# Head norms by a product with a block of ones, modulation columns by transposes, experts gathered by twos

## What is computed

```python
def rms_norm(x, g):                       # over a head (64 or 256 wide) or a latent (256, 128)
    y = x * lax.rsqrt(jnp.mean(x * x, axis=-1, keepdims=True) + EPS)
    return y * g
D_MODEL, SEQ, DEPTH, N_ADA = 1024, 256, 2, 9
N_EXPERTS, TOP_K, EXPERT_FF = 8, 2, 3584  # each of 256 tokens goes to its two best experts
```

## Time and profile before

| | |
|---|---|
| runs | 3294.65, 3297.51, 3300.77 us |
| profiled execution | 3293.94 us, span 3292.1 us |
| mean granted TensorE clock | 0.963 |
| TensorE busy | 3153.1 us, 96% |
| VectorE, ScalarE busy | 2261.7 us (69%), 1701.9 us (52%) |
| read from HBM | 734.95 MB |

### The profile page before, as it was taken

One profiled execution on the slowest core, in us unless ns is written; L12 is line 12 of the kernel. 1 busy time (PEld: TensorE's weight loads), 2 busy tenths in 40 slices (PEclk: granted clock), 3 DMA queues, 4 the chain that ended last, 5 costly groups with the idle time before them and its releaser, 6 DMA issues.

```text
span 3292.1 us, 49368 instructions
## 1 busy us (share of the span) xinstructions
PE 3153.1 (96%) x21206; PEld 2908.7 (88%) x21206; DVE 2261.7 (69%) x2574; ACT 1701.9 (52%) x1910; POOL 84.8 (3%) x163
## 2 busy tenths in 40 slices
PE   6999899999998999999989999999999999989999
PEld 6999899999988998899978888888888888889999
DVE  6686667677555555454575888888888888544575
ACT  4434343443534335443434777777777777444453
POOL 1010001011000000000000000000000000000000
PEclk9999899999988999999987999999999999989999
DMA  7685458678421653245412988989889889423353
GB/s 278 239 305 206 145 193 289 221 278 293 171 71 65 218 203 124 70 144 184 167 39 88 368 338 341 363 338 362 342 337 365 337 341 364 153 103 129 104 192 116
DMA packets 112319, 739.26 MB, mean 225 GB/s; under 512 B 12480, under 2 KB 12480, under 8 KB 32096
## 3 DMA queue, kind: packets, MB, share of 16 engines
q1 hardware_dynamic: 89424, 651.21, 53.1%
q0 software_dynamic: 22672, 84.84, 7.2%
HBM read 734.95 MB, written 1.05 MB: 224 GB/s over the span
## 4 chain that ended last, share of the span: by engine, by line
PE 79%; DVE 5%; ACT 2%; issue 1%; DMA 0%; DVEq 0%; ACTq 0%; POOLq 0%
PE ps L514 60%; PE ps L513 17%; PE ps L523 2%; DVE wlo L2702 2%; DVE AF L2684 1%; ACT whi L1823 1%; DVE att L2693 0%; DVE hl L2675 0%; DVE gf L2687 0%; ACT cv L1811 0%; DVE T L2675 0%; DVE AF L2675 0%; ACT hh L1811 0%; ACT L1811 0%; ACT AF L1811 0%
## 5 line engine op out<-in xcount | busy, mean ns | idle before, releaser
L2702 DVE TENSOR_TENSOR wlo<-ring,whi 128x2048 fp32r<-128x2048 f32 x620 | 1418.7, 2291 | 505.9 <-ACT whi L1823 505.5
L1823 ACT ACTIVATE whi<-ring 128x2048 fp32r<-128x2048 f32 x620 | 1186.0, 1915 | 342.9 <-issue 236.0
L514 PE MATMUL ps<-whi,AR 128*128 128x512 f32 (+1 forms) x2724 | 880.2, 398 | 0.4 <-DVE AF L2675 0.4
L514 PE MATMUL ps<-hh,whi 128*128 128x256 f32 x2464 | 707.5, 287 | 3.9 <-DVE wlo L2702 3.3
L514 PE MATMUL ps<-hl,whi 128*128 128x256 f32 x2464 | 701.3, 285 | 0.0
L514 PE MATMUL ps<-hh,wlo 128*128 128x256 f32 x2464 | 701.3, 285 | 0.0
L514 PEld LDWEIGHTS ps<-whi,AR 128*128 128x128 f32 x2724 | 511.7, 188 | 117.9 <-DVE AF L2675 0.9
L514 PE MATMUL ps<-wlo,AR 128*128 128x512 f32 (+1 forms) x1362 | 536.9, 394 | 0.0
L514 PEld LDWEIGHTS ps<-hh,whi 128*128 128x128 f32 x2464 | 476.1, 193 | 8.6 <-DVE wlo L2702 3.5
L514 PEld LDWEIGHTS ps<-hl,whi 128*128 128x128 f32 x2464 | 476.3, 193 | 0.1
L514 PEld LDWEIGHTS ps<-hh,wlo 128*128 128x128 f32 x2464 | 475.6, 193 | 0.2
(11 more groups left out here) (218 smaller groups left out, 3322.1 us busy)
## 6 DMA issues: line engine op xcount, KB each, us to landing
ring<-in_w SPq DMA_DIRECT2D x620, 1024.0 KB, 4.9
rring<-in_r POOLq DMA_DIRECT2D x151, 512.0 KB, 4.7
AF<-in_mem POOLq DMA_DIRECT2D x2, 1024.0 KB, 6.1
X<-in_x POOLq DMA_DIRECT2D x1, 1024.0 KB, 14.0
AF<-in_cst POOLq DMA_DIRECT2D x1, 1024.0 KB, 5.4
y_out<-X SPq DMA_DIRECT2D x1, 1024.0 KB, 3.8
cst<-in_cst POOLq DMA_DIRECT2D x1, 608.5 KB, 4.4
sm<-in_small POOLq DMA_DIRECT2D x1, 378.0 KB, 4.6
```

What stands on the lines that cost most here:

```text
L514: return self.e.matmul(out, l, r, start=start, stop=stop)
L1823: self.e.activation(N.whi[:, c % HB, :], N.ring[:, c % RING, :], ACT.Copy).then_inc(N.sem["hi"], 1)
L2702: self.e.tensor_tensor(N.wlo[:, c % HB, :], N.ring[:, c % RING, :], N.whi[:, c % HB, :].bitcast(F32), ALU.subtract).then_inc(N.sem["lo"], 1)
```

## The change

- Head norms: one matmul with a 128x128 block matrix of ones (`pairs`, or all ones in `cross` and `hybrid`) gives the sums already spread over the partitions; root and reciprocal then work over the whole tile, in place, in one of three slots of `gs`. `rows_of`, `bcast`, `rows_out`, `rT` go.
- Modulation columns: four transposes and a reduction on VectorE in place of the four matmuls with a column of ones.
- Experts: one selection matrix for two experts; `gather` is run for pairs, with 256 columns per matmul, and the first slice of an odd expert comes before the even one's matmuls back.
- A constant `SLOTS = 3` is put before `LOADS`, and used for the slots of `gs`. `SLOTS = 128` (L24), `experts` and `second` are not in the diff.

```diff
@@ constants
-    put("ex", ex.reshape(4, -1))
+    put("pairs", (i[:, None] // 64 == i[None, :] // 64).astype(np.float32))
@@ -130,6 +126,7 @@
+SLOTS = 3
 LOADS = ("cst", "small", "x", "mem", "pos", "rot3", "pool3", "mem3")
@@ Net
-        self.gs = sb("gs", [P, 2, 512])
+        self.gs = sb("gs", [P, SLOTS, 512])
@@ lay
-        self.e_zeh, self.e_zel = ar.take(8, P), ar.take(8, P)
-        self.e_Sel = ar.take(2, P)
+        self.e_Sel = ar.take(2, 2 * P)
         self.o_Sel = ar.take(2, P)
         af = Arena(self.AF)
         af.n = ar.n
+        self.e_zeh, self.e_zel = ar.take(2, 8, P), ar.take(2, 8, P)
@@ Side
+    def slot(self, key):
+        return self.N.gs[:, self.count.slots[key] % SLOTS, :]
@@ Pe
+    def wide_sum(self, key, weights, tiles, last=1):
+        b = self.take((key, "ss"))
+        self.wait_ge("act", (key, "sq", last))
+        for k, x in enumerate(tiles):
+            t = self.mm(b[:, 0:x.shape[-1]], weights, x, k == 0, k == len(tiles) - 1)
+        t.then_inc(*self.up((key, "ss")))
@@ Pe.ada_sums
         for i in range(4):
-            t = self.mm(b[:, i:i + 1], self.acc[:, g % 2, i * P:(i + 1) * P], N.ones[:, 0:1], True, True)
+            t = self.tr(b[:, i * P:(i + 1) * P], self.acc[:, g % 2, i * P:(i + 1) * P])
@@ Pe.pair_stat
-        self.stat(key, [sq[:, 0:S], sq[:, S:2 * S]], self.N.C("half"))
+        self.wide_sum(key, self.N.C("pairs"), [self.next_slot(key)])
@@ Pe.gather
-        for g in range(2):
+        for g in range(4):
             for lo, z in enumerate((N.hh2, N.hl2)):
                 b = self.take((ex, "ze", g, lo))
-                for j in range(4):
-                    k = 4 * g + j
+                for j in range(2):
+                    k = 2 * g + j
                     for tb in range(2):
-                        t = self.mm(b[:, j * P:(j + 1) * P], z[:, tb, k * P:(k + 1) * P], Sel[:, tb, :], tb == 0, tb == 1)
+                        t = self.mm(b[:, j * S:(j + 1) * S], z[:, tb, k * P:(k + 1) * P], Sel[:, tb, :], tb == 0, tb == 1)
@@ Pe.expert
-        up(0)
-        up(1)
+        if ex % 2 == 0:
+            up(ex, 0)
+        up(ex, 1)
...
-        if ex < 7:
+        if ex % 2 == 0:
+            up(ex + 1, 0)
+        elif ex < 7:
             self.gather(ex + 1)
@@ Act
+    def wide_root(self, key, div, out=None):
+        out = self.slot(key) if out is None else out
+        self.wait_ge("mm", (key, "ss"))
+        self.act(out, self.ps((key, "ss"))[:, 0:out.shape[-1]], ACT.Sqrt, (key, "sqrt"), ("free", (key, "ss")), scale=1.0 / div,
+                 bias=self.N.C("eps"))
@@ Act.pair_squares
-        if r >= 2:
-            self.wait_ge("mm", (self.sqs[r - 2], "ss"))
+        if r >= SLOTS:
+            self.wait_ge("dve", (self.sqs[r - SLOTS], "h", 1))
@@ Dve.ada_sums
-        self.tt(N.mod[:, l, m], self.ps(("ada", g))[:, 0:4], N.V("ada_b", l)[:, m], ALU.add, ("free", ("ada", g)))
+        turned = self.ps(("ada", g)).rearrange("p (a b) -> p a b", a=4)
+        self.e.tensor_reduce(out=cols, in_=turned, axis=AX, op=ALU.add).then_inc(*self.up(("free", ("ada", g))))
+        self.wait_ge("dve", self.here())
+        self.tt(cols, cols, N.V("ada_b", l)[:, m], ALU.add)
@@ Dve
+    def wide_inv(self, key, out=None):
+        out = self.slot(key) if out is None else out
+        self.wait_ge("act", (key, "sqrt"))
+        self.rec(out, out, (key, "inv"))
@@ Dve.pair
+        inv = self.slot(key)
+        self.wait_ge("dve", (key, "inv"))
         for k in range(2):
-            self.stt(x[:, k, :], x[:, k, :], gain, self.ps(bc)[:, 0:S], ALU.mult, ALU.mult, (key, "h", k), ("free", bc))
+            self.stt(x[:, k, :], x[:, k, :], gain, inv[:, k * S:(k + 1) * S], ALU.mult, ALU.mult, (key, "h", k))
@@ Dve.select, two experts at a time
+        for i in range(2):
+            for tb in range(2):
+                at = slice(ex + i, ex + i + 1)
+                self.ts(N.e_Sel[:, tb, i * P:(i + 1) * P], N.C("iota")[:, 0:P], RK[:, tb, at], M[:, tb, at], ALU.is_equal,
+                        ALU.mult, *([(ex, "sel")] if i and tb else []))
```

More of the change, by code:

```diff
@@ L294, in lay @@
         af.n = ar.n
+        self.e_zeh, self.e_zel = ar.take(2, 8, P), ar.take(2, 8, P)
+        self.e_gh, self.e_gl = ar.take(3, 256), ar.take(3, 256)
+        self.e_SelT = [ar.take(S) for _ in range(4)]
+        self.e_yh, self.e_yl = ar.take(1024), ar.take(1024)
+        assert ar.n <= self.AF.shape[1]
         self.o_w = [af.take(CH), flat2(self.T)]
@@ L403, in __init__ @@
         self.seen, self.held = {}, {}
-        self.row, self.rt, self.base, self.span = {}, {}, 4, 4
+        self.row, self.base, self.span = {}, 4, 4
         self.sq, self.sqs = 0, []
@@ L564, in start, with stat @@
         self.wait_ge("act", "consts")
-    def stat(self, key, tiles, inds=None):
+    def stat(self, key, tiles):
         n = len(tiles)
@@ L570, in stat, with stat_part @@
         self.take((key, "ss"))
-        self.stat_part(key, tiles, range(n), inds)
-    def stat_part(self, key, tiles, part, inds=None):
+        self.stat_part(key, tiles, range(n))
+    def stat_part(self, key, tiles, part):
         n, b = len(tiles), self.ps((key, "ss"))
@@ L942, in hybrid @@
         self.lin(("hy", "u", 0), [(0, name, (0,), 0, 8, (0, 256))], "hy")
-        self.stat("hyq", [T4[:, k, :] for k in range(2)])
-        self.stat("hykv", [N.T[:, 0, :]])
+        self.wide_sum("hyq", N.ones[:, :], [T4[:, k, :] for k in range(2)])
+        self.wide_sum("hykv", N.ones[:, :], [N.T[:, 0, :]], 0)
         self.lin(("hy", "gc", 0), [(0, name, (0,), 0, 8, (512, 256))], "hy")
@@ L1169, in nsa, with next_slot @@
         self.new_x()
[L1171 to L1176, removed]
-    def pair_stat(self, key):
-        sq = self.N.gs[:, self.sq % 2, :]
-        self.sq += 1
-        self.stat(key, [sq[:, 0:S], sq[:, S:2 * S]], self.N.C("half"))
[L1185 to L1190, removed]
+    def next_slot(self, key):
+        self.count.slots[key] = self.sq
+        self.sq += 1
+        return self.slot(key)
+    def pair_stat(self, key):
+        self.wide_sum(key, self.N.C("pairs"), [self.next_slot(key)])
     def memory(self):
@@ L1370, in conv_layer @@
         lin("g", 0)
-        self.stat("cvm", [N.T[:, k, :] for k in range(2)], N.C("half"))
+        self.wide_sum("cvm", N.C("pairs"), [flat2(N.T[:, 0:2, :])])
         lin("a", 0)
-        self.pair_rows("cvm")
         lin("g", 1)
-        self.pair_bcast("cvm")
         lin("a", 1)
@@ L2617, in cross @@
         lin("k", 1)
-        self.root("k0", 256)
+        self.wide_root("k0", 256, self.slot("k0")[:, 0:S])
         self.root("x3", 1024)
@@ L2628, in cross @@
         val(0)
-        self.root("k3", 256)
+        self.wide_root("k3", 256, self.slot("k3")[:, 0:S])
         self.chunk()
@@ L2644, in rest @@
             self.chunk()
-            self.root("q3", 256)
+            self.wide_root("q3", 256, self.slot("q3")[:, 0:S])
             val(1)
@@ L3706, in expert @@
         for n in range(2):
-            if ex < 7:
-                self.gathered(ex + 1, n)
+            if ex % 2 and ex < 7:
+                self.gathered(ex + 1, 2 * n)
+                self.gathered(ex + 1, 2 * n + 1)
             h = N.e_yh[:, n * 512:(n + 1) * 512]
@@ L3819, in normed @@
             v, key = {"q": N.a_q, "k": N.a_k}[n][:, 2 * h:2 * h + 2, :], f"{n}{h}"
-            self.scaled_rows(key, v, v, gain, 2, lambda k: (key, "n", k))
-            self.mark((key, "h"))
+            self.wait_ge("dve", (key, "inv"))
+            for k in range(2):
+                self.stt(v[:, k, :], v[:, k, :], gain[:, k:k + 1], self.slot(key)[:, 0:S], ALU.mult, ALU.mult, (key, "h", k))
         self.chunk()
         self.chunk()
-        self.rinv("k0")
+        self.wide_inv("k0", self.slot("k0")[:, 0:S])
         self.rinv("x3")
         self.chunk()
-        self.rinv("k1")
+        self.wide_inv("k1", self.slot("k1")[:, 0:S])
         self.chunk()
@@ L3835, in cross @@
         normed("k", 1, gk)
-        self.rinv("k3")
+        self.wide_inv("k3", self.slot("k3")[:, 0:S])
         self.chunk()
```

327 lines of the change are left out of this document (123 added, 204 removed).

## The result

The changed kernel takes 4985.49 us (median of 4, 4982.58 to 4993.31), against 3299.14 for the kernel before (3294.65 to 3302.51, 4 runs): ratio 1.511, 95% interval 1.5086 to 1.5132. What the change was meant to improve did improve, by 44 us; the constant bound twice cost 1732 (experiments 1 and 2).

The account below looks back on a forecast made before the run. The prediction took TensorE to bound the kernel (busy 96% of the span, 79% of the chain). 3293.9 us, −45 for the wanted part and +1900 for the second pass gave 5149, stated as 5150 us, range 4950 to 5550.

Parts of the forecast that it names:

- The part that decides: Guard in `experts`: `SLOTS` bound again as 3 opens it whatever the data, all eight experts run `second`, +1900 us.
- The slice at full clock: One slice of the second pass: period of 14.4 us from matmuls, chunk landings and the chain over the engines.
- One expert at full clock: One expert of the second pass: 217 us without any lowered clock, or +1740 us for the pass.
- the best case of the forecast: Second pass at full clock, +1740 us, with a saving of 65 us elsewhere: 4970 us, chance 0.17.
- the low end: Whole kernel: 4950 us, from full clock, the largest saving and 20 us for shorter handovers.
- I take 0.85: Clock in the second pass: 0.85, the mean of seven stretches about the convolution, making the slice 15.7 us.
- Gathering: Experts' main pass: gathering by twos, 4.3 us for 7.0 per pair, four times, −11 us.
- Modulation columns: Modulation columns: transposes instead of matmuls save TensorE time 36 times, −16 us; VectorE gains reductions of some 0.7 us.
- Head norms: Head norms: −17 us for 14 norms, −5 for cross attention and hybrid, −12 for waits, +16 for wide reciprocals.
- The cost that I had put at 16: Wide reciprocals of the head norms on VectorE: 61 us more work, taken as 16 us, bounds 0 to 50.
- The jump of 2.4 us at the guard: Guard before the experts: TensorE's idle 2.4 us at the jump over the second pass goes, part of −12 for waits.
- the rival of later landings from ScalarE's queue: Second pass: loads land after 5.5 us, clock 0.66, slice 18.9 us, +2290; 5550 us at most, chance 0.20.

Follow-up runs that it names:

- experiments 1 and 2: Changed kernel with its new constant renamed, guard closed: 3253.14 us; kernel before with its guard comparing with 3, guard open: 5028.27 us.
- experiment 4: Changed kernel with a third chunk buffer in the second pass and its loads issued ahead of the silu and the copy: 4765.08 us.
- experiment 3: Changed kernel with three chunk buffers instead of two in the second pass, order of load issues unchanged: 4904.44 us.
- experiment 9: Changed kernel, guard open, with half of the up products left out of the second pass, loads and waits kept: 4979.70 us.
- experiment 1: Changed kernel with its new constant renamed, so the guard compares with 128 again and the second pass is skipped: 3253.14 us, ratio 0.986.

## Why the prediction was right, and which term was off

- **The part that decides** held as written: the later binding of `SLOTS` opens the guard, `second` runs for all eight experts, and nothing of it shows in the figures that the change was about. Experiments 1 and 2 show it from both sides (1732 and 1731 us).
- **The slice at full clock**, 14.4 us, was measured at 14.19. The matmuls of a chunk (3.54; 3.47 where experiment 4 runs them without a gap), the landing (4.8) and the start of half 1 (8.5 after the down step, measured 8.54) were right; the chain took 2.1 for my 2.3. A detail was off: I had chunk 0 issued just before the down step and landing at 4.9, and it leaves half a microsecond earlier, so that the two landings don't quite tie. The change doesn't feel it; experiment 3 did.
- **One expert at full clock**, 217 us (+1740), was 216.3, and the pass +1732, or 8 x 216.5. What I called the best case of the forecast, full clock, with 0.17, is the case that came, with a saving of 44 in place of its 65. The measured time lies inside the range because the low end was built on this case.
- **The step that failed** is "I take 0.85": the clock of the pass. It was read from seven stretches around the convolution with a like busy share, and the pass was granted 0.98. The price of that step is 8 x (237.5 − 217) = 164 us, of the 165 by which the forecast was over. That a broken rhythm can cost clock was right: in experiment 9 an emptier one is granted 0.84, and a piece of work lasts 1.7 times as long. What failed was the transfer. Most of the stretches of the convolution had a single long standstill of TensorE in them, as in this row of before, in the second of the seven:

```profile
1641.68 0.58 PE L523 MATMUL ps<-cst,st 128*4 128x128 f32 x2 [4.49 <-DVE st L2690]
```

  The 3.07 us before 1653.41, the 3.88 before 1677.33 and the 2.64 before 1705.81 are of the same kind. A slice is idle for 2.66 of its 14.18 us, but in four short waits, 0.79 and 0.38 us for landings and 0.93 and 0.56 in the chain, and the longest for a landing within any expert of the pass is 1.24. Only the turn has a standstill like theirs, 4.87 us, and there the clock fell too. That this difference is the reason fits the rows; no run changes it alone.
- **Gathering**: −11 forecast, −14.1 alone, with 6 us to either side. **Modulation columns**: −16 forecast, −16.4; the reduction took 0.68 us for my 0.7.
- **Head norms**: −17 − 5 − 12 + 16 = −18 forecast, −16.7. In it, the reciprocals took 3348 and 1750 ns for my 3.4 and 1.8 us, a slope of 6.2 ns a column for my 6.3. The cost that I had put at 16 came out at 21 to 23.5, with 9 us to either side; if so, the rest of the norms' change gave some 4 to 6 us more than my −34, and the two misses cancel. The jump of 2.4 us at the guard, which I counted as gone, is not: in experiment 1 TensorE stands 2.37 us before the first matmul of the gather (1767.32) and 2.45 before the next (1770.13). I had also read it wrongly: of the 4.8 us from the count to the gather TensorE fills 2.4 with matmuls on the tile `warm`, and only the 2.38 after them are idle. Together the terms gave −45 for a measured −44, which is in part luck. An estimate from the Trainium skill (VectorE: DVE Perf Modes, First, the fixed hardware budget: an iterative divide repeated 8 times; 4.3 us for 512 columns at the page's clock) is further off than the slope of the trace.
- **Landings**: the rival of later landings from ScalarE's queue falls: the median of 336 is 4.8 us. The 6.15 us of the Trainium skill (DMA: Bandwidth & Descriptors, Bandwidth), which it gives for loads issued from GpSimd, would have put the period at 17.1 with the other terms as forecast; the measurement decides against it here.

## What to carry to other kernels

A constant is part of the control flow of everything that compares with it: before any instruction is priced, look for every reader of a name that a diff binds anew. When a pass without a trace must be priced, lay out one period event by event from rows. Then ask of the clock which waits and which unbroken pieces of work that period has, and keep full clock as a case in its own right, since a stretch of the same busy share elsewhere says little. A wide, slow operation off the critical engine can cost the critical one: here leaving 64 us of reciprocals out of VectorE saved 21 to 23.5 us of the whole, and placing them later in its order won back at most some 8. Whether the same result from narrower rows is cheaper was not tried.

## What was not expected of the hardware

- Leaving out a third of a pass's matmuls (half of the up products; 896 of 2688 records) saved nothing: 4979.70 for 4985.49 us. The clock fell from 0.98 to 0.84, and the mean record of this group rose from 618 to 747 ns:

```profile
L510 PE MATMUL ps<-AF 128*128 128x512 f32 x896 | 541.2, 747 | 246.9 <-DMA AF<-in_w 219.8 <-ACT AF L2380 27.1
```

- Removing the waits for landings left the clock where it was: with the loads issued early (experiment 4) the pass stood at 0.98, as in the change. The short waits of a slice had cost it nothing, and it still fell at the turns of expert.

```profile
1800.00:3200.00 1400.00, 1225.11 (x3094) 553.11 (x3093) 66.69 (x146) 100.24 (x250) 0.00 (x0) 0.98 0.64 235
```

- A reciprocal of 512 columns (3.35 us) costs VectorE nearly five of the reductions over as many columns (0.68), and the width is what is paid: 2 columns took 0.166 us. A way to the reciprocal that keeps the narrow rows and still spreads them by one product was not tried.
